# Reordering a few instructions inside the mixer slots of a decoder-block kernel: two unfoldings, one state update, the key transposes and the transposes of the normalised rows

## Time and profile before

| | us |
|---|---|
| median of 3 runs (lowest, highest) | 2169.05 (2166.82, 2170.37) |
| profiled execution, its own time | 2167.59 |
| span of the profile | 2165.9 |
| PE busy | 2134.2 (99%) |
| DVE busy | 1364.3 (63%) |
| ACT busy | 843.6 (39%) |
| POOL busy | 432.5 (20%) |

### The profile page before, as it was taken

How to read it: one execution, slowest core, us unless ns; L and a number is a source line. 1 busy time by engine, 2 the same in 40 slices (tenths; PEclk the granted TensorE clock), 3 DMA queues, 4 the chain that set the end, 5 groups by cost and what they waited for, 6 DMA issues and landing times.

```text
span 2165.9 us, 28872 instructions
## 1 busy us (share of the span) xinstructions
PE 2134.2 (99%) x10708; PEld 1778.9 (82%) x10708; DVE 1364.3 (63%) x2136; ACT 843.6 (39%) x1628; POOL 432.5 (20%) x403
## 2 busy tenths in 40 slices
PE   8999999999999999999999999999999999999998
PEld 7878888888888888788888887888888888888886
DVE  5886477547754776766566765568755556564556
ACT  5343342324232423444333333356433333333445
POOL 2342022102210221222233230000222233210000
PEclk9999999999999999999999999999999999999999
DMA  7666754664467437543355657887433323237666
GB/s 247 227 231 209 264 183 145 198 223 179 146 196 229 171 132 235 217 148 115 107 209 214 218 191 234 261 267 253 172 101 102 106 89 122 93 105 236 225 208 228
DMA packets 215740, 402.48 MB, mean 186 GB/s; under 512 B 16944, under 2 KB 100912, under 8 KB 211760
## 3 DMA queue, kind: packets, MB, share of 16 engines
q1 hardware_dynamic: 215600, 400.63, 54.6%
HBM read 292.04 MB, written 108.53 MB: 185 GB/s over the span
## 4 chain that ended last, share of the span: by engine, by line
PE 87%; DVE 5%; issue 4%; DMA 2%; ACT 1%; POOL 1%; SPq 0%; DVEq 0%; ACTq 0%; POOLq 0%
PE M L1282 10%; PE M L1284 10%; PE M L1283 10%; PE M L971 6%; PE M L973 6%; PE M L972 6%; PE M L1307 3%; PE M L1309 3%; PE M L1308 3%; PE X L1309 3%; PE X L1308 3%; PE X L1307 3%; PE X L1284 3%; PE X L1282 3%; PE X L1283 3%
## 5 line engine op out<-in xcount | busy, mean ns | idle before, releaser
L2292 DVE TENSOR_TENSOR ring_lo<-ring_raw,ring_hi 128x1024 fp32r<-128x1024 f32 x154 | 189.7, 1232 | 162.6 <-ACT ring_hi L1707 162.1
L1707 ACT ACTIVATE ring_hi<-ring_raw 128x1024 fp32r<-128x1024 f32 x154 | 163.3, 1061 | 230.4 <-DMA ring_raw<-a_scr 225.5
L1282 PE MATMUL M<-t_hi,wu_hi 128*128 128x512 f32 x616 | 240.2, 390 | 0.3 <-DVE wu_lo L2180 0.3
L1284 PE MATMUL M<-t_hi,wu_lo 128*128 128x512 f32 x616 | 239.9, 390 | 0.0
L1283 PE MATMUL M<-t_lo,wu_hi 128*128 128x512 f32 x616 | 239.7, 389 | 0.0
L971 PE MATMUL M<-uhi,split 128*128 128x512 f32 (+1 forms) x528 | 206.6, 391 | 2.9 <-DVE ulo L1843 2.9
L973 PE MATMUL M<-uhi,split 128*128 128x512 f32 (+1 forms) x528 | 202.9, 384 | 0.0
L972 PE MATMUL M<-ulo,split 128*128 128x512 f32 (+1 forms) x528 | 202.4, 383 | 0.0
L2180 DVE TENSOR_TENSOR wu_lo<-fraw,wu_hi 128x512 fp32r<-128x512 f32 x132 | 124.0, 948 | 123.3 <-ACT wu_hi L1649 122.9
L2557 POOL TENSOR_TENSOR fs<-fraw 128x512 f32<-128x512 f32 x43 | 61.0, 1418 | 415.8 <-DMA fraw<-in_w_gate_dram 208.5
L2477 POOL TENSOR_TENSOR pr<-pr,rd 128x256 f32<-128x256 f32 x64 | 44.6, 697 | 459.1 <-DVE rd L1854 459.1
(11 more groups left out here) (312 smaller groups left out, 5012.6 us busy)
## 6 DMA issues: line engine op xcount, KB each, us to landing
split<-w_scr SPq DMA_DIRECT2D x60, 1024.0 KB, 5.6
ring_raw<-a_scr SPq DMA_DIRECT2D x154, 256.0 KB, 3.6
w_scr<-split SPq DMA_DIRECT2D x30, 1024.0 KB, 6.5
split_next<-w_scr SPq DMA_DIRECT2D x30, 1024.0 KB, 5.0
fraw<-in_w_gate_dram SPq DMA_DIRECT2D x44, 512.0 KB, 4.8
fraw<-in_w_up_dram SPq DMA_DIRECT2D x44, 512.0 KB, 4.8
a_scr<-au SPq DMA_DIRECT2D x88, 256.0 KB, 2.4
ring_raw<-t_scr SPq DMA_DIRECT2D x88, 256.0 KB, 3.0
```

The source lines that it names most:

```text
L1282: mm(bank[:, :], wh[:, k, :], hi[:, k, :], start=start and k == 0, stop=False, skip_group_check=True)
L1284: last = mm(bank[:, :], wl[:, k, :], hi[:, k, :], start=False, stop=k == KH - 1, skip_group_check=True)
L1707: A(hi[:, :, :], raw_r[:, :, :], ACT.Copy).then_inc(s_rowhi, 1)
L2292: V.tensor_tensor(lo[:, :, :], raw_r[:, :, :], hi[:, :, :].bitcast(F32), ALU.subtract).then_inc(s_rowlo, 1)
```

## The change

Four orders are changed. No instruction is added or removed, no buffer and no semaphore.

1. On PE, `key_turn` of heads 0, 1 and 2 moves from behind the group of slots 8, 13 and 18 into its middle, ahead of the thirteenth of its 24 matmuls. That of head 3, in slot 22, stays.
2. On PE, `u_turn` (slots 18 to 25, iterations 1 to 3) moves ahead of `update`, `iv_turn` and `keys` of its slot.
3. On DVE, `unfold` of step 1 moves to the end of slot 5, behind `gateq`, `qdec` and the first reciprocal; that of step 9 moves from slot 13, where it stood ahead of the state update, to slot 14, behind the normalisation of head 1 and ahead of the scaling L2162.
4. On DVE, the state update of head 2 in slot 18 moves from behind the running product of head 3 to ahead of it, behind `forget`.

```diff
+UNFOLD_LATE = (5, 13)
 ...
-            def group(it, slot):
+            def group(it, slot, head=None):
 ...
                 for k in range(KD):
+                    if head is not None and k == KD // 2:
+                        key_turn(it, head)
 ...
-                        group(it, slot)
+                        group(it, slot, head_at(slot, UPDATE))
 ...
-                    a = head_at(slot, UPDATE)
-                    if a is not None and slot != OUT_A:
-                        key_turn(it, a)
 ...
+                    if it and 0 <= slot - UT_SLOT < 2 * TB:
+                        u_turn(it - 1, slot - UT_SLOT)
                     for offset, step in ((UPDATE, update), (V_TURN, iv_turn), (KEYS, keys)):
                         a = head_at(slot, offset)
                         if a is not None:
                             step(it, a)
-                    if it and 0 <= slot - UT_SLOT < 2 * TB:
-                        u_turn(it - 1, slot - UT_SLOT)
 ...
                     dve.wait_ge(s_f, n + 1)
+                    if a == HEADS - 1:
+                        update(it, a - 1)
                     if a >= 2:
                         dve.wait_ge(s_kst, n - 1)
                     for c in range(NCH):
 ...
-                        unfold(it, i)
+                        if slot not in UNFOLD_LATE:
+                            unfold(it, i)
 ...
                     for offset, step in ((KEYS, keys), (UPDATE, update), (NORM_SUM, head_sum)):
                         a = head_at(slot, offset)
-                        if a is not None:
+                        if a is not None and (step is not update or slot != F_SLOT[-1]):
                             step(it, a)
+                    for late, i in ((5, 1), (14, 9)):
+                        if slot == late:
+                            unfold(it, i)
```

## The result

| | before | changed |
|---|---|---|
| median, us (22 runs each) | 2168.07 | 2173.23 |
| lowest, highest | 2166.46, 2170.52 | 2170.20, 2175.39 |
| profiled execution (span) | 2167.59 (2165.9) | 2170.20 (2168.5) |

The ratio is 1.0021 with an interval of 1.0015 to 1.0028: the change makes the kernel slower by about 0.2%, 5.2 us between the medians, a little more than the 4.3 us that the forecast called "no change that can be measured". The forecast was 2169.9, within a range of 2165.2 to 2174.2. It started from a median of before of 2169.05 over 3 runs; over 22 it is 1.0 lower.

A forecast was written before the change was run, and what follows sets the result against it. PE, busy 99% of the span, was the bound, with 11.2 us of waits reachable. Iteration 0 +1.4, iterations 1 to 3 -0.9, breaking +0.6 less 0.3: +0.8, forecast median 2169.9, range 2165.2 to 2174.2.

The forecast's parts named there:

- The stands: PE waits for `iv` mid-group: 0.98, 1.5, 3.35 us in slots 8, 13, 18 of iteration 0; 0.84 in later slots 18.
- Iteration 0: Sum for the first iteration: +0.9 to slot 14, +1.9 in slot 18, -1.4 in slot 19, together +1.4 us.
- a sign that it is wrong: Prediction counts as wrong if iteration 0 takes over 3 us more or less, or later slots 18 lack L1132 waits.
- Iterations 1 to 3: Sum for the later iterations: 3 x (-0.4 + 0.1) = -0.9 us, with group breaking counted separately.
- The 0.83: PE's slot 14 wait for the states, iterations 1 to 3: removed by moving unfolding 9, lost again by slot 18; net 0.
- The 0.4 an iteration: Slots 13 to 17: DVE up to 0.4 us earlier, `kst` eviction being out of ACT's way; bounds 0 and 0.5.
- the breaking of their nine groups: Splitting a group costs 0.1 us, twelve times over all iterations, half coming back: 0.6 in all, bounds 0 and 1.2.
- The unfolding beside POOL: Slot 14, iteration 0: unfolding 9 falls beside POOL's 2.41 us pass, taken as not held; if held, DVE loses 1.2.
- The update of slot 22 behind `u_turn`: `u_turn` first delays slot 22's update by 0.4 us, so 0.1 of wait arises; bounds 0 and 0.4.
- The escape from POOL: First rival, faster: `nm` in slot 17 starts before POOL's pass, `iv` 1.1 to 1.4 us earlier; 2164.4, chance 0.11.
- The rival of stands that are not given back: Second rival, slower: mid-group waits delay ACT and DVE, waits of slots 14 and 19 stay; +6.5, 2175.6, chance 0.16 with halfway cases.
- the last paragraph of the rivals: Behind the 3.35 us stand the group might run at 1.2 GHz, doubling its 5.7 us once; assigned to the slower side.

The follow-up runs named there:

- the filling: The changed kernel plus 13 unread 128x512 matmuls ahead of the key transposes of slot 18, iteration 0: 2170.75 us, ratio 1.0007 to before.
- the second set: The changed kernel, unaltered, timed again beside its variant with extra matmuls in slot 18, against the kernel before: 2173.45 us, ratio 1.0015.

## Why the forecast was too small, though right in most of its steps

The forecast was slower by 0.8 us, "no change that can be measured"; the result is slower by 5.2, a little more than that. The direction is the same, the size is not.

- **The stands.** Said: 1.0, 1.5 and 3.4 in iteration 0 and 1.1 (0.84 in the working) in slot 18 of the others. Measured: 0 (hidden by the slow clock), 1.32, 3.12, and 1.00. Together 7.5 against "some 9". Right but for slot 8.
- **Iteration 0.** Slot 8 cost 1.64 instead of 0.98, slot 13 1.56 (1.5), and the output of slot 14 gave 1.6 back: the states decided, as said, with 0.18 left of the wait. Slot 18 cost 1.96 (1.9) and slot 19 gave back 1.6 (1.44). From slot 7 to the end the delay grows by 4.0 - 1.3 = 2.7 against 1.4. The rest of the difference is the clock in slot 8 and 0.8 in slots 9 to 12, where the key product waits 0.73 instead of 0.17. Iteration 0 as a whole took 4.0 us more, over the 3 us that the prediction named as a sign that it is wrong; 1.3 of them stand ahead of slot 7.
- **Iterations 1 to 3.** The 0.83 doesn't stay won, as argued. The 0.4 an iteration that I counted from the eviction of `kst` did arrive at `iv`: in slot 17 of iteration 1 it comes with a delay of 3.29 where the iteration began with 3.62. But only 0.18 is left at the start of slot 19 (3.44), and slots 19 to 23 take more than that (3.70 at the end). So each iteration ends under 0.1 later instead of 0.3 earlier. In the sum iterations 1 to 3 stood at -0.9, and the profile has +0.2 from 3.62 on, 1.1 us more; some of it is the breaking of their nine groups, which the sum has elsewhere.
- **The unfolding beside POOL.** It takes 1.22 us at 138.77, beside a POOL pass of 2.42 that starts at 138.45, so it isn't held, and `den` behind it is held for 0.99 instead of 2.10 (0.9 was said). The timeline of POOL and DVE, iteration 0, slot 14, in the changed kernel:

```profile
138.45 2.42 POOL L2501 TENSOR_TENSOR split<-raw,split 128x1024 fp32r<-128x1024 f32 x1
...
138.77 1.22 DVE L1892 TENSOR_TENSOR pT<-X,keep 128x1024 int32<-128x1024 int32 x1
139.90 0.99 DVE L1850 TENSOR_TENSOR den<-rs,es 128x2 f32<-128x2 f32 x1
```

- **The update of slot 22 behind `u_turn`.** 0.1 of wait was said for slot 23. The list of waits has none, but PE loses 0.16 there in iteration 1 (the delay goes from 3.55 to 3.71 around the first output matmul, which starts at 419.17; the seventh state ends at 419.12): as said, and too small for the list.
- **The escape from POOL.** It didn't come: `nm` still starts with POOL's pass, at 374.76 and 374.71.
- **The rival of stands that are not given back.** The time came within 2.4 us of its 2175.6, but by another way: it was to decide from a wait of over 1 us in slot 14, and that is 0.18.

**The step that failed** is the last paragraph of the rivals. It said that a stand of 3.35 us is longer than any wait now, that the group behind it could run at 1.2 GHz and that "its 5.7 us would double once", and it put this only on the slower side. In the sum the clock stood at nothing. Measured it is 2.5 us in one profile (a half group at half speed), 1.6 in another, nothing in two, and 2.4 (1.3 to 3.6) from the filling. The second term that was off is the working from slot 7 to the end of the mixers: forecast +0.8, in the profile 3.8 - 1.3 = 2.5, of which 0.7 is the clock in slot 8. With 1.0 to 2.4 for the clock behind slot 18 this makes 3.5 to 4.9, against 5.2 measured, and 4.1 in the second set. That the time still fell into the range is not to the sum's credit: it counted on a kernel whose clock stays at 1.00.

A stand is thus priced twice: by its length, and by what the clock does behind it. The Trainium skill ("TensorE: Matmul & The Clock Gate", Part 1) ties the clock to how busy the engine was; the rows agree in that the filled stand keeps 1.00, though two of the four unfilled ones keep it too.

What stays open: what decides whether the clock falls behind the same stand, how often it does in the change and in the kernel before (of which there is one profile, with 1.00 behind slot 7), and the 0.8 of slots 9 to 12.

## What to carry to other kernels

Before a dependent instruction is moved into the middle of work that waits for nothing, put the time of its last operand beside the time of its new place in every iteration, the first above all: here the same move costs about 7 us in the middle of the group (5.2 + 1.5) and wins 2 ahead of its last three matmuls. A new stand of 2 to 3 us on TensorE is to be priced with the slow stretch behind it, and one profile doesn't tell whether that comes: take a second one, and compare the profiled execution with the median of the runs before differences of a few us are read from the trace. Where such a stand can't be removed, matmuls that nobody reads may be cheaper than the idle time.

## What the runs showed of the hardware that was not expected

- The same stand is followed by either clock. Behind the stand of slot 7 (2.1 us, in three profiles 2.5) the window 71 to 80 us had a granted clock of 0.81 or 0.82 in 8 of the 13 profiles without filling, and 1.00 in 5; filled it had 1.00. Behind the 3.1 us stand of slot 18 (window 163 to 171 us) it was 1.00 in two profiles, 0.58 in one and 0.79 in one. Elsewhere, in all 14 profiles, the clock is below 1.00 only near 12 us, among the waits of the start-up, and in the last 10 us.
- Work added into a stand made the kernel faster: 13 matmuls (3.11 us) by 2.4 us, eight (2.11 us) by 2.3.
- Breaking a group into another bank costs almost nothing: the matmul behind the transposes shows 0.48 us, its neighbours 0.39, and the kernel with twelve groups broken ahead of their last three matmuls is the fastest but one of all that were run.
- A DVE instruction of two columns waits for a long POOL pass as long as that pass lasts: `den` takes 0.99 when it comes 1.45 us into the pass and 2.10 when it comes 0.32 into it; alone, it takes 0.10 to 0.16.
